# A transformer layer on one core: y loaded whole into g's place, and the sample's value product turned round

## The reference

```python
h = rmsnorm(x, norm_mix_g[l])
u = jnp.einsum('btd,dc->btc', h, w_in[l])
# four mixers (RG-LRU, SSD, gated delta, S5) turn u into y_a, y_b, y_c, y_d
mix = jnp.concatenate([y_a, y_b, y_c, y_d], axis=-1)
x = x + jnp.einsum('btc,cd->btd', mix, w_out[l])
x = x + cross_attend(rmsnorm(x, norm_cross_g[l]), mem_k, mem_v, w_cq[l], w_co[l])
x = x + swiglu(rmsnorm(x, norm_ffn_g[l]), w_ffn_gate[l], w_ffn_up[l], w_ffn_down[l])
```

```python
p = jax.nn.softmax(s, axis=-1)
o = jnp.einsum('bhtm,bmhe->bhte', p, v)
```

## Time and profile before

| | us |
|---|---|
| median of 3 runs | 3968.19 (3960.0 to 3970.13) |
| the profiled execution | 3968.14 |
| its span, first to last instruction | 3966.4 |
| TensorE busy | 3585.8 (90%) |
| VectorE busy | 2192.2 (55%) |
| ScalarE busy | 1349.8 (34%) |
| mean granted TensorE clock | 0.944 |

### The profile page before, as it was taken

One profiled execution on the slowest core, in us unless ns is written; L12 is line 12 of the kernel. 1 busy time (PEld: TensorE's weight loads), 2 busy tenths in 40 slices (PEclk: granted clock), 3 DMA queues, 4 the chain that ended last, 5 costly groups with the idle time before them and its releaser, 6 DMA issues.

```text
span 3966.4 us, 67837 instructions
## 1 busy us (share of the span) xinstructions
PE 3585.8 (90%) x26310; PEld 3422.0 (86%) x26310; DVE 2192.2 (55%) x4725; ACT 1349.8 (34%) x2489; POOL 96.8 (2%) x319
## 2 busy tenths in 40 slices
PE   6779787888978999888999998999998999989998
PEld 6768786788878999888999988899988899989998
DVE  6556754358765666663655572655573555554323
ACT  5453434234534342422322332322332332322101
POOL 2200001000000000000000000000000000000000
PEclk9989897789989999999999999999999999999999
DMA  6767567657777677777566567566667465566776
GB/s 221 236 221 253 196 209 247 199 188 234 251 245 280 240 277 250 268 239 250 195 228 217 201 236 277 194 230 225 216 218 278 164 219 181 201 227 246 247 252 213
DMA packets 370432, 909.60 MB, mean 229 GB/s; under 512 B 34624, under 2 KB 173504, under 8 KB 369728
## 3 DMA queue, kind: packets, MB, share of 16 engines
q1 hardware_dynamic: 370112, 905.27, 66.5%
HBM read 730.56 MB, written 174.57 MB: 228 GB/s over the span
## 4 chain that ended last, share of the span: by engine, by line
PE 51%; issue 19%; DVE 12%; DMA 6%; ACT 5%; DVEq 3%; SPq 2%; POOLq 1%; ACTq 1%; POOL 0%; PEldq 0%; PEld 0%
PE banks L465 14%; PE banks L466 13%; PE banks L467 13%; PE banks L1623 2%; DVE wlo_sb L1127 2%; DMA wlo_sb<-kept_dram 2%; ACT whi_sb L935 1%; DMA kept_dram<-wlo_sb 1%; PE banks L883 1%; DMA ldb_sb<-y_dram 1%; DVE uc_sb L1219 1%; DVE m_p_sb L2230 1%; DVE m_p_sb L2200 1%; PE banks L1593 1%; DVE hl_sb L1146 1%
## 5 line engine op out<-in xcount | busy, mean ns | idle before, releaser
L465 PE MATMUL banks<-hh_sb,whi_sb 128*128 128x384 f32 (+1 forms) x3360 | 1157.4, 344 | 104.2 <-DVE wlo_sb L1127 29.7
L466 PE MATMUL banks<-hh_sb,wlo_sb 128*128 128x384 f32 (+1 forms) x3360 | 1122.0, 334 | 0.0
L467 PE MATMUL banks<-hl_sb,whi_sb 128*128 128x384 f32 (+1 forms) x3360 | 1120.6, 334 | 0.0
L465 PEld LDWEIGHTS banks<-hh_sb,whi_sb 128*128 128x128 f32 x3360 | 652.2, 194 | 134.8 <-DVE wlo_sb L1127 37.4
L466 PEld LDWEIGHTS banks<-hh_sb,wlo_sb 128*128 128x128 f32 x3360 | 653.5, 194 | 1.6 <-issue 0.5
L467 PEld LDWEIGHTS banks<-hl_sb,whi_sb 128*128 128x128 f32 x3360 | 651.5, 194 | 0.0
L465 PE MATMUL banks<-g_hi_sb,whi_sb 128*128 128x384 f32 (+2 forms) x1504 | 512.4, 341 | 57.5 <-DVE x_sb L1324 27.4
L466 PE MATMUL banks<-g_hi_sb,wlo_sb 128*128 128x384 f32 (+2 forms) x1504 | 497.6, 331 | 0.0
L467 PE MATMUL banks<-g_lo_sb,whi_sb 128*128 128x384 f32 (+2 forms) x1504 | 497.2, 331 | 0.0
L1324 DVE TENSOR_TENSOR x_sb<-x_sb,banks 128x384 f32<-128x384 f32 (+2 forms) x400 | 201.6, 514 | 281.7 <-PE banks L467 273.2
L465 PEld LDWEIGHTS banks<-g_hi_sb,whi_sb 128*128 128x128 f32 x1504 | 291.4, 194 | 73.0 <-DVE x_sb L1324 31.5
(11 more groups left out here) (442 smaller groups left out, 4916.9 us busy)
## 6 DMA issues: line engine op xcount, KB each, us to landing
whi_sb<-kept_dram SPq DMA_DIRECT2D x504, 512.0 KB, 3.9
wlo_sb<-kept_dram SPq DMA_DIRECT2D x504, 512.0 KB, 5.1
raw_sb<-w SPq DMA_DIRECT2D x176, 512.0 KB, 5.2
kept_dram<-whi_sb SPq DMA_DIRECT2D x112, 512.0 KB, 5.4
kept_dram<-wlo_sb SPq DMA_DIRECT2D x112, 512.0 KB, 6.4
uc_dram<-uc_sb SPq DMA_DIRECT2D x90, 192.0 KB, 2.7
ldb_sb<-x_t SPq DMA_DIRECT2D x64, 192.0 KB, 4.5
plain_sb<-w SPq DMA_DIRECT2D x32, 256.0 KB, 5.0
```

Of the source, the lines that this page charges most:

```text
L465: eng.matmul(out, xh, yh, start=first, stop=False)
L466: eng.matmul(out, xl, yh, start=False, stop=False)
L467: return eng.matmul(out, xh, yl, start=False, stop=last)
```

## The change

1. **y at once.** At the four boundaries behind a `z` section, y is no longer loaded into `ldb`. SP issues four DMAs of two tiles each into `g_free`, the room of `g_hi` and `g_lo`, which is unused at that time, all on one semaphore `y_loaded`. ACT copies tiles 0 to 6 to `hh` ahead of the eviction of the last `z` product, and tile 7 behind it. Each copy waits for all four DMAs, and for `h_used` as before.
2. **The last low half.** Where an `up` section is followed by `d`, DVE makes `g_lo` in the `up` section itself, ahead of the mixer step.
3. **The sample's values.** In `sv` the 32 columns of probabilities are the weights and the 256 columns of the cache tile move, two products per sequence instead of four, in the form of `ss`. The result has tokens on its partitions. ACT copies it to `pr` (two copies), and a new section `su` turns it round with four transposes and writes it to `g_free`. Heads 2 and 3 get columns of their own there, and the list is `sv0 sp1 ss2 su0 sv1 sp2 ss3 su1 sv2 sp3 so so su2 sv3 so so su3 so so so so`.
4. **Semaphores.** `setup_rot` and `state_done` are dropped, and their waits go to higher counts of `setup_inv` and `begun`.

```diff
-            out += [sv[0], sp[1], ss[2], sv[1], sp[2], ss[3]] + rows("so", 0)
-            out += [sv[2], sp[3], sv[3]] + rows("so", 1)
+            out += [sv[0], sp[1], ss[2], su[0], sv[1], sp[2], ss[3], su[1], sv[2], sp[3]] + so[:2]
+            out += [su[2], sv[3]] + so[2:] + [su[3]] + rows("so", 1)
...
         def h_source(item):
+            if item.early >= 0:
+                return g_free[:, item.k // 4, item.k % 4, 0:h_cols(item)]
...
             n, src = h_cols(item), h_source(item)
-            if item.kind in "AMYQ":
+            if item.early >= 0:
+                eng.wait_ge(y_loaded, 64 * item.early + 64)
+            elif item.kind in "AMYQ":
                 eng.wait_ge(ld_loaded[item.ld % LDS], 16 * LD_LOADS[item.ld])
...
             if s.kind == "z":
                 for j in range(tiles(s.p)):
+                    if j == tiles(s.p) - 1:
+
+                        for item in s.preps[:-1]:
+                            act_prep(eng, item)
                     out = act_slot(eng, s.q + j)
...
-            for item in s.preps:
+            for item in s.preps[-1:] if s.kind == "z" else s.preps:
                 act_prep(eng, item)
...
+        def sp_early(eng, items):
+
+            eng.wait_ge(full, G_LAST[items[0].early])
+            p = items[0].p
+            n, t0 = cols(p), PASSES[p][0] * P
+            for out in ("y_l", "y_x", "y_s", "y_g"):
+                eng.wait_ge(ms[out], 16 * PASSES[p][1])
+            for q in range(4):
+                eng.dma_start(g_free[:, q // 2, q % 2 * 2:q % 2 * 2 + 2, 0:n],
+                              y_dram[:, 2 * q:2 * q + 2, t0:t0 + n]).then_inc(y_loaded, 16)
...
             elif after_mixer(s):
-                sp_tiles(eng, s.preps[:LDS])
+                sp_early(eng, s.preps) if s.preps[0].early >= 0 else sp_tiles(eng, s.preps[:LDS])
...
-                for e in range(2):
-                    for mt in range(2):
-                        o = e * P + j * SEQ_LEN
-                        c = j % 4 * 32
-                        last = eng.matmul(bank[:, o:o + SEQ_LEN], kv_slot(n)[:, 2 * mt + e, :],
-                                          pt[:, mt, j // 4, c:c + SEQ_LEN], start=mt == 0, stop=mt == 1)
+                r = slice(j % 4 * 32, j % 4 * 32 + 32)
+                out = bank[r, j // 4 * 256:j // 4 * 256 + 256].rearrange("p (a b) -> p a b", a=2)
+                for mt in range(2):
+                    last = eng.matmul(out, pt[:, mt, j // 4, r], kv_slot(n)[:, 2 * mt:2 * mt + 2, :],
+                                      start=mt == 0, stop=mt == 1)
...
+        def pe_sample_rows(eng, s):
+
+            eng.wait_ge(av_done, s.a + 1)
+            bank = pe_bank(eng, s.f)
+            for e in range(2):
+                for sh in range(2):
+                    o = (2 * e + sh) * P
+                    last = eng.transpose(bank[:, o:o + P], pr[:, 3 * sh, e * P:e * P + P], ident)
+            last.then_inc(full, 1)
...
             elif s.kind == "sv":
                 bank = bank_in(eng, s.f)
+                if s.a:
+                    eng.wait_ge(full, SU_FILL[s.a - 1] + 1)
+                for sh in range(2):
+                    last = eng.activation(pr[:, 3 * sh, :], bank[:, sh * 256:sh * 256 + 256], ACT.Copy)
+                last.then_inc(av_done, 1)
+                eng.drain().then_inc(free[s.f % 3], 1)
...
                 eng.tensor_tensor(gf[:, s.a % 2, 0:n], gs[:, s.a % 2, 0:n], bank[:, 0:n], ALU.mult).then_inc(up_done, 1)
                 eng.drain().then_inc(free[s.f % 3], 1)
+                if taken_next(i):
+                    dve_g_low(eng, s)
```

More of the change, by code:

```diff
@@ L256, in schedule @@
         if secs[-1].kind == "z":
-            spread(secs[-1:], preps("Y", p, hy))
+            items = preps("Y", p, hy)
+            for x in items:
+                x.early = early
+            early += 1
+            spread(secs[-1:], items)
         else:
@@ L312, in schedule @@
         for x in s.preps:
-            if x.kind in "AMYQ":
+            if x.kind in "AMYQ" and x.early < 0:
                 x.ld, ld = ld, ld + 1
@@ L331, in schedule @@
             s.kv, kvn = kvn, kvn + SEQS
-        made = {"k": [s.a % 4], "pt": [s.a % 2 * 2, s.a % 2 * 2 + 1], "sv": [s.a % 2 * 2, s.a % 2 * 2 + 1],
+        made = {"k": [s.a % 4], "pt": [s.a % 2 * 2, s.a % 2 * 2 + 1], "su": [s.a % 2 * 2, s.a % 2 * 2 + 1],
                 "up": [(s.a - sum(BLOCKS[:s.b])) if s.kind == "up" else 0]}.get(s.kind, [])
@@ L335, in schedule @@
             s.g = g
-            s.gfree = tuple(slot_fill.get(t, 0) for t in made)
+            s.gfree = su_free if s.kind == "su" and s.a else tuple(slot_fill.get(t, 0) for t in made)
+            if s.kind == "su":
+                su_free = s.gfree
             for t in made:
@@ L352 @@
 N_LD = len(LD_PREP)
+G_LAST = {x.early: max(o.f + o.nf for o in SECS[:i] if o.gneed) for i, s in enumerate(SECS) for x in s.preps if x.early >= 0}
 H_LAST = {s.hi: i for i, s in enumerate(SECS) if s.hi >= 0}
@@ L369 @@
 SV_FILL = {s.a: s.f for s in SECS if s.kind == "sv"}
+SU_FILL = {s.a: s.f for s in SECS if s.kind == "su"}
 def stored(q, slot):
@@ L645, in program @@
         ld_loaded = [sem(f"ld_loaded{s}") for s in range(LDS)]
+        y_loaded = sem("y_loaded")
         sq_done, sq_used = sem("sq_done"), sem("sq_used")
@@ L790, in pe_sample_out @@
                         eng.wait_ge(g_hi_done, s.gneed[k])
-                    last = eng.matmul(bank[:, 0:P], w[:, k, dd * P:dd * P + P], g_free[:, 0, k, 0:P],
+                    last = eng.matmul(bank[:, 0:P], w[:, k, dd * P:dd * P + P], sample_tile(2 * s.a + k // 2, k % 2),
                                       start=k == 0, stop=k == 3)
@@ L1222, in dve_taps, with taken_next, dve_g_low @@
             last.then_inc(conv_done, 1)
+        def taken_next(i):
+            return SECS[i + 1].kind == "d"
+        def dve_g_low(eng, s):
+            slot, n = s.a - sum(BLOCKS[:s.b]), cols(s.p)
+            eng.wait_ge(g_hi_done, s.g + 1)
+            eng.tensor_tensor(g_lo[:, slot, 0:n], gf[:, s.a % 2, 0:n], g_hi[:, slot, 0:n].bitcast(F32),
+                              ALU.subtract).then_inc(g_lo_done, 1)
         def dve_second(eng, i):
@@ L1240, in dve_second @@
                 eng.drain()
[L1241 to L1246, removed]
+            elif s.kind == "up" and not taken_next(i):
+                dve_g_low(eng, s)
+            elif s.kind == "su":
                 eng.wait_ge(g_hi_done, s.g + 2)
```

30 lines of the change are left out of this document (20 added, 10 removed).

## The result

| | before | after |
|---|---|---|
| median of 4 runs each, us | 3969.01 (3960.0 to 3970.13) | 3928.01 (3922.98 to 3929.88) |
| the profiled execution, its span, us | 3968.14, 3966.4 | 3928.61, 3926.7 |
| TensorE busy, us | 3585.8 | 3555.5 |
| mean granted TensorE clock | 0.944 | 0.949 |

The account below looks back on a forecast made before the run. TensorE's busy time and its waits were taken as the bound; DVE and ACT count only where TensorE waits for them. 3968.1 - 11.6 (part 1) - 0 (part 2) - 20 (part 3) = 3936.5 us, range 3914 to 3955.

Parts of the forecast that it names:

- pass 2: First w section after z: the ring's wait goes, weights land 2.9 us later, section ends at 1812.8; gain 2.8 us.
- pass 3: Same boundary in pass 3: new start at 2417.5, end at 2422.5 to 2423 against an eviction at 2427.28; gain 4 us.
- pass 4: Same boundary in pass 4: weights land 2.9 later at 3033.5, end at 3039.5 with the clock penalty; gain 2.5 us.
- pass 0: Boundary where x is late: SP gets past y sooner, x loads at 591.8, w eviction at 601.1; gain 2.3 us.
- the recorded reading: At pass 3's boundary in before, a low part was waited for at 2415.50 (2.00 us), not the weights.
- the 2 us taken: Clock penalty at pass 2's boundary: half of the first w section at half speed after TensorE's idle adds 2 us.
- weights are not delayed: Rival: y does not push the weights back, or the clock stays up; part 1 gives 33 us, 3915; chance 0.14.
- the boundary gains nothing: Rival: weights or x come so late that they replace the ring's wait; part 1 gives 0 to 2, 3947; chance 0.13.
- the 5 us for longer landings: Sample's new sv sections: slower landing of the eighth tile adds 1.7 us to each of four, 7 in all, 5 taken.
- The 5.2 us of the earlier trace: Issue to landing of a tile in a loaded stretch, put against some 3.5 us for the eighth cache tile.
- The slower rival: The new sv's four groups of 32 output partitions do not overlap: 71 us in all, 3981; chance 0.04.
- The cache stream sets the pace: Rival: back-to-back ss and sv wait for each of eight tiles, 10 us a section; gain 6, 3950; chance 0.11.

Follow-up runs that it names:

- the second execution: The kernel after, unchanged, run again in a later job beside the split behind the eviction: 3923.94 us, against 3928.01 in its first runs.
- the kernel of part 1 alone: The kernel before with only y at once added, no change to the last low half or the sample's values: 3958.15 us, ratio 0.9975.
- the kernel with x first: The kernel after with pass 0's four x loads issued ahead of the last z section's stores: 3918.09 us, ratio 0.9874.
- the split behind the eviction: The kernel after with all eight ACT copies of y behind the last z eviction: 3920.69 us, and 3919.77 when run again.
- eight slots: The kernel after with eight slots for the sample's cache tiles instead of seven: 3910.30 us, ratio 0.9850.
- y earlier: The kernel after with y's four loads issued one z section earlier, behind that section's weights: 3908.95 us, ratio 0.9849.

## Why the prediction was right, step by step

**What bounds the kernel.** Right: DVE's and ACT's work did not change, and the time followed TensorE's busy time and its waits.

**Part 1, 11.6 forecast, 11.4 measured alone.** By boundary in the trace, from the end of z to the first w eviction: pass 2 4.1 us (2.8 forecast), pass 3 2.0 (4), pass 4 2.7 and another 1.0 in the next section (2.5), pass 0 2.4 (2.3): 12.2. (At pass 0 that is 586.37 to 603.36 in before and 587.62 to 602.17 in after. By the time in the trace the eviction came only 1.2 earlier, since z ended 1.25 later in after.) The mechanism held: the ring's wait went, the weights came later. That the sum came out within 0.2 is in part luck, for its terms were off against each other. TensorE idled 3.55, 5.59 and 5.25 at passes 2 to 4, where the steps gave 5.9, 4.0 and 6.1. Against the idle time of before, 3.03, 2.00 and 3.19, the first weights were delayed by 0.5, 3.6 and 2.1 us; with the second execution and the kernel of part 1 alone the nine delays are 0.5 to 3.6, 1.8 in the mean, where 2.9 had been put. At pass 3 the recorded reading is wrong as well: the weights had no slack in before. The weight load's row names them, and they landed at 2415.3 (issued at 2408.58, 6.7 us), level with the low part (2415.35):

```profile
2415.47 0.19 PEld L465 LDWEIGHTS banks<-hh_sb,whi_sb 128*128 128x128 f32 x1 [2.17 <-DMA wlo_sb<-kept_dram]
```

The y tiles were put some 5 us before the weights, but the first copy started only 2.6 us before TensorE, and it cost nothing. In the second execution of after the matmul's row names a low part, which looks like a wait for y; but the first low part was there at 1770.2, and the weight load's row of the same moment names the weights (issued at 1762.58, 9.1 us to landing, 1771.7). The last line is the window behind it:

```profile
1771.68 0.69 PE L479 MATMUL banks<-hh_sb,whi_sb 128*128 128x384 f32 x1 [5.03 <-DVE hl_sb L1192]
...
1771.68 0.29 PEld L479 LDWEIGHTS banks<-hh_sb,whi_sb 128*128 128x128 f32 x1 [5.24 <-DMA wlo_sb<-kept_dram]
...
1771.60:1775.00 3.40, 3.32 (x10) 0.50 0.62 183
```

And the clock cost more than the 2 us taken: the blocks of passes 2 to 4 took 7.2, 6.2 and 6.7 us, 3.1, 2.1 and 2.6 over the 4.1 at full clock. The rival "weights are not delayed" fell, and so did "the boundary gains nothing".

**Pass 0.** The forecast had the last z eviction near 590 and the x loads at 591.8. They were at 589.94 (eviction) and 592.23, and the eviction of w came 9.9 us after them, not 9.3: 602.17 for 601.1. Both steps held; the kernel with x first shows that the order on SP was the price, and the split behind the eviction that holding z's store behind seven copies cost 1.3 to 2.6 us of it.

**Part 2.** 0 forecast, nothing seen.

**Part 3, 20 forecast; 25.3 in the trace, 28.7 measured alone.** By its terms, forecast and found in this stretch: `sv` 49.45 - 24.1 - 5 = 20.3, found 49.45 - 22.9 = 26.6 (sections of 5.1, 6.0, 6.7 and 5.1; the windows above, rounded out, add to 23.2); `su` -3.3, found -3.0; the wait of `so` for `su` 3 -1, found -2.8; the two `ss` sections of the stretch 0, found -0.6; the clock +4, found 5.1, which is what is left of 25.3 (everything else in the stretch at a mean clock of 0.85 instead of 0.65, 1.0 of it a shorter wait for DVE). So the term that was mis-sized is the 5 us for longer landings; the wait for `su` 3 was 1.8 us longer than put, the other way. The 5.2 us of the earlier trace rows did not become waits: the gaps were 2.1, none, 1.3 and 2.1, never longer than those of `ss`. The cache stream did speed up about as forecast: from the first `sv` to the last it came at 241 GB/s, where before had 185 and 248 had been put. (Busy of PE, PEld, DVE, ACT, POOL; clock; DMA share; GB/s.)

```profile
743.50:797.30 53.80, 45.11 (x417) 27.38 (x408) 14.66 (x45) 11.60 (x35) 0.00 (x0) 0.90 0.86 241
```

The nine executions with seven slots (after twice, and seven of the kernels above) took 77.9 to 81.3 us from the first `sv` to the last `so`, 25.3 to 28.7 less than before, which is how 25.3 and 28.7 go together. With the 12.2 of the boundaries, 37.5 of the 39.7 us of the span are placed. The slower rival fell: the four groups of 32 outputs overlap, and 32 instructions were busy 3.00 us, not 32 x 0.35. The new sections ran at a clock of 0.93 to 1.00, the second of before at 0.50. "The cache stream sets the pace" gave 6 us where 25 came.

The Trainium skill (TensorEngine Tiling (Array Packing), Key Properties) has a change of tiling mode drain TensorE. The trace shows how little room there is for it. `sv` of heads 1 to 3 stands directly behind the full-width transposes of `su`, and starts at 762.03, 777.81 and 792.12, each 0.07 to 0.08 before the modelled end of the last transpose. In heads 2 and 3 a transpose starts 0.13 behind the one before it, and the first row of `sv` 0.20 behind the last transpose (estimates, from four transposes in 0.66 us, each 0.27 long). So such a drain costs less than 0.1 us here, by this estimate.

**Open.** The gains of the kernels with eight slots and with y earlier, against the first median of after, are 5 to 7 us more than their own places show; against the second they are 1 to 3 more. The scatter of one execution, up to 10 us in the middle (1788.24 and 1778.52), covers it, but the medians of four runs do not settle it. Why the first weights came 0.5 us later at one boundary and 3.6 at another is not shown either.

## To carry to other kernels

When a load that is waited for is moved, look at what then stands second in the same queue: at these boundaries y and the weights only changed places as the last to come, and the real gain was to start y sooner, while the DMAs had room. A ring of n slots that feeds sections of n + 1 tiles makes most sections wait for the last tile (1.3 to 2.3 us here), and one more slot can be worth nearly half of what the cheaper inner product gave (here 11 us shown beside 25). Take an unseen cost from the rows of the same form (`ss` gave the new `sv` within 1.3 us of 24.1), and don't add to it what those rows already hold. Where a matmul's wait names an engine that had long been done, look at the weight load's row too.

## What the runs showed of the hardware

- Instructions of plain float32 products with 32 columns of weights and 256 moving, in four groups of output partitions, overlap: in `sv` 0 28 instructions took 1.95 us, 0.07 each, where the four of the late tile took 1.05.
- After 3.55 us of idle, at the end of which the clock had begun to fall (0.70), TensorE ran at 0.50 for the next 6 us (1781 to 1787), though it was busy all that time. After 1.76 us of idle, with y earlier, it ran at full clock for 1 us and at 0.51 for the next 3, busy all the time (stretch, length, busy PE, clock, DMA share, GB/s):

```profile
1770.20:1771.20 1.00, 0.97 (x5) 1.00 1.03 340
1771.20:1774.20 3.00, 3.00 (x11) 0.51 1.07 385
```

- Two executions of the kernel after were 2.1 us apart at 600, 9.7 at 1780 and 7.1 at 3525, with all its runs between 3921.21 and 3929.88.
